# A first stage in which four column chunks are begun on four K-tiles and finished later, two-block transformer kernel

## The reference

```python
c_act = jax.nn.silu(c)
mod = c_act @ w_ada[l] + b_ada[l]              # w_ada: 2048 x 12288
sh_m, sc_m, gt_m, sh_f, sc_f, gt_f = jnp.split(mod[:, None, :], N_MOD, axis=-1)
h = rmsnorm(x, pre_mix_norm[l]) * (1.0 + sc_m) + sh_m
proj = h @ w_in[l]                             # w_in: 2048 x 8208
o_hg = hgrn2_group(proj[..., :HG_COLS], ...)   # columns 0..4095
o_gdn = gdn_group(proj[..., HG_COLS:], ...)    # a causal convolution over columns 4096..7167, gates, norms
```

## Time and profile before

| | before |
|---|---|
| time of the runs, median of 3 | 2758.19 us (2754.61, 2758.19, 2760.06) |
| span of the profiled execution | 2752.8 us |
| PE busy | 2666.5 us, 97% |
| DVE busy | 1794.1 us, 65% |
| ACT busy | 1215.7 us, 44% |

### The profile page before, as it was taken

The page is one execution under the profiler, slowest core; times in us unless marked ns, Lnnn a source line. Parts: engine busy times, 40 slices in busy tenths (PEclk is TensorE's granted clock), DMA queues, the critical chain, the costliest instruction groups (busy, mean ns, idle before and its releaser), DMA issues.

```text
span 2752.8 us, 32675 instructions
## 1 busy us (share of the span) xinstructions
PE 2666.5 (97%) x12618; PEld 2164.2 (79%) x12618; DVE 1794.1 (65%) x2202; ACT 1215.7 (44%) x1548; POOL 69.3 (3%) x92
## 2 busy tenths in 40 slices
PE   5999999899999999999999999999999999999998
PEld 3478887687888888888887778788888888888896
DVE  7888677995786555555577355667665565656576
ACT  2145635443444443444344454544654434353443
POOL 1000000001000000000000100000000000000000
PEclk9999999999999999999999999999999999999999
DMA  9988888345595555555574644444455555555553
GB/s 376 369 270 273 298 303 283 126 181 217 203 352 191 189 184 185 189 188 185 189 291 163 196 153 139 139 166 159 162 198 180 191 187 192 183 185 181 198 172 119
DMA packets 166944, 571.73 MB, mean 208 GB/s; under 512 B 9993, under 2 KB 30648, under 8 KB 162609
## 3 DMA queue, kind: packets, MB, share of 16 engines
q1 hardware_dynamic: 161936, 544.25, 57.7%
q0 software_dynamic: 4720, 25.57, 2.5%
q10 hardware_dynamic: 176, 0.40, 0.0%
HBM read 562.58 MB, written 7.60 MB: 207 GB/s over the span
## 4 chain that ended last, share of the span: by engine, by line
PE 59%; issue 28%; DVE 9%; ACT 2%; DMA 2%; POOL 0%; SPq 0%; DVEq 0%; POOLq 0%; ACTq 0%
PE banks L475 16%; PE banks L477 16%; PE banks L476 16%; DMA raw_weights<-in_w_ada 2%; PE banks L932 2%; DVE mod_in L1019 1%; PE banks L592 1%; DVE weights_low L437 1%; ACT weights_high L424 1%; DVE modulation L455 1%; DVE proj L1388 1%; DVE proj L1231 1%; PE banks L893 1%; PE banks L1945 0%; DVE proj L1215 0%
## 5 line engine op out<-in xcount | busy, mean ns | idle before, releaser
L437 DVE TENSOR_TENSOR weights_low<-raw_weights,weights_high 128x1024 fp32r<-128x1024 f32 (+2 forms) x814 | 966.3, 1197 | 726.7 <-ACT weights_high L424 719.0
L424 ACT ACTIVATE weights_high<-raw_weights 128x1024 fp32r<-128x1024 f32 (+2 forms) x814 | 838.7, 1037 | 959.5 <-PE banks L477 903.3
L475 PE MATMUL banks<-weights_high,lhs_high 128*128 128x512 f32 (+1 forms) x2264 | 898.9, 397 | 10.3 <-DVE weights_low L437 3.9
L477 PE MATMUL banks<-weights_high,lhs_low 128*128 128x512 f32 (+1 forms) x2264 | 882.0, 390 | 0.0
L476 PE MATMUL banks<-weights_low,lhs_high 128*128 128x512 f32 (+1 forms) x2264 | 880.7, 389 | 0.0
L475 PEld LDWEIGHTS banks<-weights_high,lhs_high 128*128 128x128 f32 x2264 | 426.5, 188 | 104.6 <-DVE weights_low L437 10.5
L477 PEld LDWEIGHTS banks<-weights_high,lhs_low 128*128 128x128 f32 x2264 | 426.2, 188 | 88.7
L476 PEld LDWEIGHTS banks<-weights_low,lhs_high 128*128 128x128 f32 x2264 | 426.8, 189 | 82.6 <-issue 1.2
L475 PE MATMUL banks<-weights_high,hid_high 128*128 128x512 f32 x768 | 300.7, 391 | 3.0 <-DVE y_rows L574 1.7
L477 PE MATMUL banks<-weights_high,hid_low 128*128 128x512 f32 x768 | 299.2, 390 | 0.0
L476 PE MATMUL banks<-weights_low,hid_high 128*128 128x512 f32 x768 | 299.1, 389 | 0.0
(11 more groups left out here) (429 smaller groups left out, 2069.3 us busy)
## 6 DMA issues: line engine op xcount, KB each, us to landing
raw_weights<-in_w_ff SPq DMA_DIRECT2D x128, 1024.0 KB, 4.9
raw_weights<-in_w_ada SPq DMA_DIRECT2D x96, 1024.0 KB, 7.1
raw_weights<-in_w_in SPq DMA_DIRECT2D x96, 1024.0 KB, 5.6
raw_weights<-in_w_up SPq DMA_DIRECT2D x80, 1024.0 KB, 5.0
raw_weights<-in_w_down SPq DMA_DIRECT2D x42, 1024.0 KB, 5.1
raw_weights<-in_w_out SPq DMA_DIRECT2D x32, 1024.0 KB, 5.1
first_weights<-in_w_in SPq DMA_DIRECT2D x16, 768.0 KB, 12.0
raw_weights<-in_w_up SPq DMA_DIRECT2D x16, 384.0 KB, 3.9
```

Source lines behind the costliest of these rows:

```text
L424: act.activation(WHI[:, u % SPN, 0:c.width], raw_unit(c, n, k), ACT.Copy).then_inc(S("high_made"), 1)
L437: dve.tensor_tensor(WLO[:, u % SPN, 0:c.width], raw_unit(c, n, k), WHI[:, u % SPN, 0:c.width].bitcast(F32), ALU.subtract).then_inc(S("low_ ...
L475: nc.tensor.matmul(o, x, hi, start=(k == 0), stop=False)
L477: mm = nc.tensor.matmul(o, y, hi, start=False, stop=(k == c.kn - 1))
```

## The change

Nothing is computed otherwise in sum; the order and the share of native and split products differ.

- The groups of K-tiles are now 4, 6 and 6. Modulation sums run over both components at once: rows of 1024 for group 0, of 1536 for groups 1 and 2 (L486, L489, tiles `key_pairs` and `modulation`).
- Natives cover K-tiles 0 to 3 of four whole chunks, 5, 4, 6, 7 (L972). The first three are put aside in `proj` by ACT; the fourth stays in the banks.
- Then come split products: chunk 7 on K-tiles 4 to 9 (`in_gate`, goes on in the same banks, then is put aside), chunks 6 and 4 on K-tiles 4 to 9 (`in_value` and the next, added to what was put aside, L615), chunk 5 on K-tiles 4 to 15 (`in_key`), chunks 4, 6 and 7 on K-tiles 10 to 15, then chunks 0 to 3 as before.
- The 16 loads of group 2's modulation columns (0.79 MB each) stand between the weight loads of the first 22 split units.
- In the convolution ACT does the first tap, DVE three of four. Its rounds, the work on `mem` and the mask cast stand elsewhere.
- The other columns of `w_ada` come as whole rows of 2048 (L496), 32 loads as before, more of them in the last chunks.

```diff
-        GROUPS = [(0, 4), (4, 4), (8, 4), (12, 2), (14, 2)]
+        GROUPS = [(0, 4), (4, 6), (10, 6)]
+        MOD_SUMS = [QK21, MOD[:, 3, 0:1536], MOD[:, 3, 0:1536]]
+        FIRST_LOADS = [(0, 2 * j, 2) for j in range(KT // 2)] + [(1, kt, 1) for kt in range(KT)]
+        FIRST_CHUNKS = (5, 4, 6, 7)
+        FIRST_AFTER = {6: 0, 7: 1, 9: 2, 12: 3, 15: 4, 17: 5, 19: 6, 21: 7}
-        segs = [(1, [in1(5, "conv0", None, 512), in1(6, "conv1", in_ada[6]), in1(7, "conv2", in_ada[7])] +
-                 [in1(j, ("gdn_silu", "gdn_norms", "gdn_values", "in1_last")[j], in_ada[j]) for j in range(4)])]
+        for x in ((), (), (), (4,), (1,), (1,), (0, 2), (1, 3, 5, 7), range(1, 8), range(8), range(8)):
+            in_ada.append({p: [divmod(sum(len(y) for y in in_ada) + n, KT)] for n, p in enumerate(x)})
+        for counts in ((1, 2, 1), (2, 1, 2), (1, 2, 1), (2, 1)):
...
+        segs = [(1, [in1(FIRST_CHUNKS[3], "in_gate", k0=G1_AT, kn=G1_N, mods=in_mods[0], cont=True),
+                     in1(K2, "in_value", k0=G1_AT, kn=G1_N, add=True, mods=in_mods[1]),
+                     in1(K1, None, k0=G1_AT, kn=G1_N, add=True, mods=in_mods[2]),
+                     in1(K0, "in_key", in_ada[3], k0=G1_AT, kn=G1_N + G2_N, add=True, mods=in_mods[3]),
+                     in1(K1, "conv_key", in_ada[4], k0=G2_AT, kn=G2_N, add=True),
+                     in1(K2, "conv_key_end", in_ada[5], k0=G2_AT, kn=G2_N, add=True),
+                     in1(FIRST_CHUNKS[3], "in_memory", in_ada[6], k0=G2_AT, kn=G2_N, add=True)] +
+                 [in1(j, ("conv_rest", "gdn_silu", "gdn_norms", "in1_last")[j], in_ada[7 + j]) for j in range(4)])]
+        segs[0][1][0].lag = segs[0][1][0].act_lag = 1
...
+                for x, kt in enumerate(c.mods_after(k // 2) if k % 2 == 1 else ()):
+                    mod_step(dve, 2, kt, n + 1 + c.ada_after(k // 2) + x)
+
+        def mod_step(dve, q, kt, m, at=0):
+
+            acc, c, done = MOD_SUMS[q], COND[:, kt:kt + 1], KT * q + kt
...
+            dve.wait_ge(S(f"weights_in{m % RAWN}"), landed(m))
...
+                dve.wait_ge(S("mod_summing"), done)
+                ins = dve.scalar_tensor_tensor(out=acc, in0=row, scalar=c, in1=acc, op0=ALU.mult, op1=ALU.add)
...
+            def piece(p):
+                ci, last = p // 2, p == PIECES - 1
...
+                    if last and j == 1:
+                        mod_columns(pe, 1)
...
+        def in_gate():
+
+            def low(k):
+                return lambda pe: pe.wait_ge(S("x_low"), k + 1)
+
+            def dve_first_low(dve):
+                dve_mod_cols(dve, Chain(dve), 1)
+                dve_input_low(dve, 4, 2)
+            return dict(pe=[low(k) for k in range(6)],
+                        act=[lambda act: act_turned_input(act, 1, 4, 3), lambda act: act_turned_input(act, 1, 7, 3)],
+                        dve=[dve_first_low, lambda dve: dve_input_low(dve, 6, 2), lambda dve: dve_input_low(dve, 8, 2)])
```

More of the change, by code:

```diff
@@ L40, with mod_loads @@
 NMASK = 2 * len(LEVELS) - 1
[L43 to L45 removed]
+def mod_loads(row, kt, *positions):
+    return {j: [(row, kt + n)] for n, j in enumerate(positions)}
 FILL_AFTER = 1
@@ L68, in ada_after, with mods_after, number @@
     def ada_after(self, j):
-        return self.mid * (j == 1) if self.mid else int(bool(self.ada) and j in self.ada)
+        return self.mid * (j == 1) if self.mid else len(self.ada.get(j, ())) if self.ada else 0
+    def mods_after(self, j):
+        return self.mods.get(j, ())
     def load_of(self, j):
-        return self.at["n"] + j + sum(self.ada_after(x) for x in range(j)) + (len(self.fill) if j > FILL_AFTER else 0)
+        return self.at["n"] + j + sum(self.ada_after(x) + len(self.mods_after(x)) for x in range(j)) + (len(self.fill) if j > FILL_AFTER else 0)
     def fill_load(self, x):
         return self.load_of(FILL_AFTER) + 1 + x
[L82 to L87, removed]
+def number(segments, first_sums):
+    u, n, done, signals = 0, len(first_sums), [3] * 4, [3, 3, 3, 0]
+    native = 8
+    rel = {m: ("mod", sums) for m, sums in enumerate(first_sums)}
+    prev = None
     ada = 0
@@ L248, in whole, with in1 @@
             return chunks
-        def in1(j, phase=None, ada=None, col0=0):
-            return ck("w_in", 0, j * UW + col0, KT, UW - col0, first, ("copy", P, j * UW + col0, 0), phase=phase, ada=ada)
+        def in1(j, phase=None, ada=None, k0=0, kn=KT, add=False, mods=None, cont=False):
+            return ck("w_in", 128 * k0, j * UW, kn, UW, [z[:, k0:k0 + kn, :] for z in first],
+                      ("add" if add else "copy", P, j * UW, 0), phase=phase, ada=ada, mods=mods, cont=cont)
         def up1(c, step=0, phase=None, ada=None):
@@ L466, in products @@
                 b = 2 * h + t
-                if k == 0 and c.at["done"][b] > 0:
+                if k == 0 and not c.cont:
                     pe.wait_ge(S(f"bank_free{b}"), val(c.at["done"][b], c.ddone[b], i))
@@ L474, in products @@
                 o = PS[:, b, 0:w]
-                nc.tensor.matmul(o, x, hi, start=(k == 0), stop=False)
+                nc.tensor.matmul(o, x, hi, start=(k == 0 and not c.cont), stop=False)
                 nc.tensor.matmul(o, x, lo, start=False, stop=False)
@@ L1039, in dve_first @@
             dve.wait_ge(S("start_mapped"), 1)
-            for n, x in enumerate(MODS[0]):
-                sums(x)
+            for n, (q, kt, rows) in enumerate(FIRST_LOADS[0:KT // 2]):
+                for j in range(rows):
+                    mod_step(dve, q, kt + j, n, UW * j)
                 if n == 1:
@@ new lines, in act_conv, with f, dve_conv @@
+        def act_conv(n, x):
+            r, c0 = conv_round(n, x)
+            def f(act):
+                act.wait_ge(S("round_ready"), r + 1)
+                for j in range(2):
+                    last = act.activation(P[:, j, c0 + 256 * x:c0 + 256 * x + T], PS[:, 4 + r % 4, 256 * j:256 * j + T],
+                                          ACT.Copy, scale=conv_columns(n, x, j, 3))
+                last.then_inc(S("conv_begun"), 1)
+            return f
+        def dve_conv(n, x):
+            r, c0 = conv_round(n, x)
+            def f(dve):
+                link = Chain(dve)
+                dve.wait_ge(S("conv_begun"), CONVS.index((n, x)) + 1)
+                for tap in (2, 1, 0):
+                    for j in range(2):
+                        sh = 3 - tap
+                        dst = P[:, j, c0 + 256 * x + sh:c0 + 256 * x + T]
+                        last = dve.scalar_tensor_tensor(out=dst, in0=PS[:, 4 + r % 4, 256 * j:256 * j + T - sh],
+                                                        scalar=conv_columns(n, x, j, tap), in1=dst, op0=ALU.mult, op1=ALU.add)
+                    if tap:
+                        link(last)
+                    else:
+                        last.then_inc(S("round_free"), 1)
+            return f
```

438 lines of the change are left out of this document (213 added, 225 removed).

## The result

The changed kernel takes 2765.74 us (median of 6 runs, 2763.33 to 2767.66), the kernel before 2757.46 us (6 runs). The ratio is 1.0033, 95% interval 1.0023 to 1.0042: 8 us slower.

What follows compares the result with a forecast made beforehand. Modulation loads bound the first part, then PE. Stage without waits 442.4, plus 12.2, 1.3 and 1.5, gives 457.4 against 463.5; span 2746.7, plus 5.4 to the median, 2752.1 us; range 2741 to 2762.

Steps and rivals of the forecast that it cites:

- What bounds the kernel: First part, to about 140 us, waits for 33.5 MB of modulation columns; from there PE is the bound.
- Natives: 64 native matmuls 56.5 us, modulation block 1.4, half clock at the start 3.2; from 42.0 they end at 103.1 us.
- What is late next: First 18 split units: PE waits 1.3 in `in_gate`, 4.9 at `in_value`, 3.2 next chunk, 2.7 at `in_key`; together 12.2 us.
- my upper bound: Waits up to `in_key`: 15 us with 6.3 us for each load, on top of 49.1 us of PE work.
- the landing: Loads in the first split units: transferred one after the other, 2.7 us (0.79 MB: 2.0), with 2.2 us behind the last byte.
- I add nothing: Half clock after the first wait falls into time in which PE would wait for DVE again; no cost added.
- DVE's work against PE's: First 18 split units: DVE's low parts, sums and chunk take 52.4 us against PE's 49.1.
- Later in the stage: Four more chunks taken out by DVE cost 1.3 us; denser loads in `gdn_norms` and `in1_last` cost 1.5 us.
- PE's other work: Stage from the first split product: 33.3 us besides the products, 34.2 - 2.3 of waits + 1.4 for last modulation products.
- C: Clock falls at each late chunk and shows: three breaks, 6.4 us in all, gain about nil, 2758; chance 0.20.
- rival D: Slower: four slots turn over at 11.1 us to landing, 78 us instead of 49, about 2766; chance 0.13.
- B: PE hardly waits, DVE catches up; the stage gains 10 to 21 us, about 2742; chance 0.25.

Runs made afterwards that it cites:

- e3_block_split: Changed kernel with group 1's 12 modulation products in two blocks of six, one ahead of each of the last two native K-tiles; 2764.07 us.
- e4_gdn_evac: Changed kernel with the banks taken out behind unit 1 instead of unit 2 in `gdn_norms` alone; 2755.91 us, ratio 1.0000 to the kernel before.
- e6_loads_small: Changed kernel with group 2's 16 loads of 64 KB instead of 768 KB each, DVE's sums kept; 2760.45 us, one execution.
- e5_sums_small: Changed kernel with DVE's 16 sums of group 2 over 16 instead of 1536 elements, loads kept; 2757.76 us, one execution.
- e7_no_group2: Changed kernel without group 2's 16 loads and 16 sums; 2742.87 us, one execution.

## Why the prediction was wrong

*What bounds the kernel* held: every microsecond of the result comes from this stage, and the first split product came 40 us earlier, at 105.07 for 103.1.

*Natives.* Two errors cancel in part. One block of 12 modulation products takes 3.11 us (2.73 at full clock), not 1.4: the trace has two records for each product, and I divided by records. Behind it the clock was at half for the last K-tile (6.68 instead of 3.5 us, in this execution). Against that the low clock at the start cost 1.3 us and not 3.2 (60 products in 54.28 us). Together 2.0 us late, and `e3_block_split`, 3.9 us earlier here and 0.05 us at `in_key`, shows that this hardly mattered.

*What is late next* is the first step that failed, in size more than in place. The waits were named at the right chunk starts and for the right reason, ACT's copy and DVE's adds behind unit 2. But the stretch to `in_key` took 66.9 us instead of 61.4, above the 64.1 of my upper bound (49.1 + 15). Two terms of the walk were too small.

One is the landing. I let each load be transferred one after the other with 2.2 us behind its last byte, 5 to 6 us from issue to use. The loads of unit 2 took 7.5 to 7.8 us with other loads under way, and 5.3 to 5.8 where those were small. That the first wait came out near, 4.3 us for 4.9, is luck: its load was issued 12.1 us behind the first split product and not 15.3, and landed 1.9 us more slowly. The next two were 4.1 us each for 3.2 and 2.7, and the 1.3 us inside `in_gate` did not come.

The other is *"I add nothing"* for the half clock. The three waits together were 12.6 us, near the 12.2 forecast; what PE lost besides is 20 matmuls at half speed, 4.0 us, and 1.2 us around them. I had argued that a slow PE would only fill a wait. But the load that ends the next wait is issued behind PE's first two units (the chain above), so that the release comes later too. From the first product of `in_value` to that issue it was 12.7 us with 14 matmuls at half speed (12.8 in `e3_block_split`, also 14), 11.3 with 6 (`e4_gdn_evac`), and 10.6 with none (`e6_loads_small`, whose other loads are small). So of the 5.5 us too much, the half clock behind the first wait made some 2, an estimate from these four traces; no run holds the clock up alone. Behind the third wait it costs 11 matmuls x 0.2 = 2.2 us. The Trainium skill (TensorE: Matmul & The Clock Gate, HAM oscillation) describes this for kernels that wait for loads; the windows above agree, 0.50 behind waits of 4.3 us. Not every wait had it: behind 3.7 us at `in_value` in `e6_loads_small` no matmul ran at half speed, behind 2.9 us at its next chunk 14 did.

I had also called it DVE's work against PE's, 52.4 against 49.1 us. `e5_sums_small` shows that with DVE's sums gone only 3.4 us come back, `e6_loads_small` that without the bytes 4.9 do. `e7_no_group2`, which frees work, bytes and slots at once, gives back 16.2 us of 17.8. That the places in the ring are the scarce thing is not shown: no run frees slots alone, and two limits, each hiding the other, would give the same three numbers.

*Later in the stage* fell short most. Two waits behind adds are there, 0.44 us each (0.9 for 1.3). But I priced the denser loads at 1.5 us, by bandwidth. They cost by the same chain as in the first chunks: at the start of `gdn_norms` unit 2's load is issued at 357.85 and used at 365.28, 7.4 us, and the copy stands behind it. PE starts 4.45 us late (from start to start; the row's 4.30 counts from the modelled end), and then 26 matmuls run at half speed, where the kernel before had 16 around its norm sums, 2.0 us. 6.4 us instead of 1.5. `e4_gdn_evac`, which moves only this copy, is 9.8 us faster.

From 457.4 to 472.0: 2.0 (natives), 5.5 (to `in_key`), 2.2 (clock behind it), 1.3 (the last modulation block, the same slip by two), 4.9 (`gdn_norms`) make 15.9 of 14.6; the surplus of 1.3 was not traced. It may lie in the 33.3 us of PE's other work, which is a remainder and not a measurement.

*The rivals.* C had a mechanism that is there: 31 matmuls at half speed behind the first three waits are 6.2 us, near its 6.4, though not all of that reached the end; its losses in the last two chunks are there too, and it had no price for them. The time is rival D's 2766, but not by its mechanism: loads did not take 11.1 us, and a good part of the loss lies at 362 us, outside its stretch. B's 2742 is what `e7_no_group2` shows without group 2 (2742.87 us). With these loads in the ring the best of the runs here is 2747.47.

## What to carry to other kernels

When loads are slipped in between others that share a small ring of slots, count the look-ahead in slots and not only in bytes: from the moment a slot is freed to the moment its content is wanted there must be the landing time under load, here 7.5 to 7.8 us, plus whatever stands behind the consumer. Shrinking the loads or the work on them gave back 4.9 and 3.4 us here, taking them out 16.2. Copying a finished accumulator out should stand behind the least that can be late; moving it one unit earlier in five chunks was two lines and worth 18 us (0.7%). When the same chain of load, split and copy stands at two places (here the first chunk starts and `gdn_norms`), price both by it. And before a slow engine is taken to fill only time in which it would wait, see whether the end of that wait hangs on this engine.

## What was not expected of the hardware

TensorE can be busy without a break in the rows and have the clock at half all the same: behind 3.1 us of one-column products the granted clock was 0.51 from 98 to 104 us, with PE 6.00 of 6 us busy. That these products are the reason is not shown. With the same block the clock did not fall there in all executions; the native K-tile behind it took 3.68, 5.06, 5.32, 5.38 or 6.68 us.
